# Squares added on GpSimd, and modulation weights in column blocks over interleaved partitions

## The reference, cut to what matters

```
c_act = silu(c)
for l in range(2):                                    # first block
    mod = c_act @ ada_w[l] + ada_b[l]                 # [1024] @ [1024, 9216]
    sh1, sc1, g1, sh2, sc2, g2, sh3, sc3, g3 = split(mod, 9)
    x = x + 0.5 * g1 * swiglu(modulate(rms_norm(x, norm_ffn1[l]), sh1, sc1), ...)
    x = x + g2 * token_mix(modulate(rms_norm(x, norm_mix[l]), sh2, sc2), ...)
    x = x + 0.5 * g3 * swiglu(modulate(rms_norm(x, norm_ffn2[l]), sh3, sc3), ...)
x = rms_norm(x, final_norm)
for i in range(2):                                    # second block, x and a context of 256 tokens
    mx = split(silu(c_2) @ ada_w_2[i] + ada_b_2[i], 6)
    mc = split(silu(c_ctx_2) @ ada_w_2[i] + ada_b_2[i], 6)
    ... attention (i = 0) or a gated linear recurrence, "LRU" (i = 1), then an MLP
```

## Time and profile before

| | before |
|---|---|
| Three runs, us | 2224.69, 2228.17, 2229.52 |
| Median, us | 2228.17 |
| Span of the profiled execution, us | 2222.6 (the page gives no other time for it) |
| PE, PEld busy | 97%, 90% |
| DVE, ACT, POOL busy | 75%, 45%, 1% |
| Moved by DMA | 417.47 MB, mean 188 GB/s |

### The profile page before, as it was taken

How to read it: one execution, slowest core, us unless ns; L and a number is a source line. 1 busy time by engine, 2 the same in 40 slices (tenths; PEclk the granted TensorE clock), 3 DMA queues, 4 the chain that set the end, 5 groups by cost and what they waited for, 6 DMA issues and landing times.

```text
span 2222.6 us, 36384 instructions
## 1 busy us (share of the span) xinstructions
PE 2155.5 (97%) x15539; PEld 1993.2 (90%) x15539; DVE 1674.6 (75%) x2327; ACT 990.5 (45%) x1331; POOL 31.1 (1%) x33
## 2 busy tenths in 40 slices
PE   7999999999999999999999899999999999999998
PEld 7999987999999998799998678888888887889998
DVE  6999877788798877778776774777776568987563
ACT  4534434534443443443344664422222348764442
POOL 0000000000000000000000000000000001110000
PEclk9999999999999999999999999999999999999999
DMA  9999744798789864467774102254465232133662
GB/s 322 317 330 309 248 133 150 242 316 298 264 284 305 302 202 153 142 196 248 236 228 142 36 4 74 80 186 155 156 221 189 76 114 69 48 122 127 223 191 76
DMA packets 338631, 417.47 MB, mean 188 GB/s; under 512 B 9274, under 2 KB 263208, under 8 KB 338472
## 3 DMA queue, kind: packets, MB, share of 16 engines
q1 hardware_dynamic: 335360, 411.84, 56.2%
q10 hardware_dynamic: 3112, 3.33, 0.5%
HBM read 414.09 MB, written 1.05 MB: 187 GB/s over the span
## 4 chain that ended last, share of the span: by engine, by line
PE 46%; DVE 7%; ACT 3%; issue 2%; POOL 0%; DVEq 0%; ACTq 0%
PE pb L623 45%; ACT wh L1461 1%; DVE wl L2100 1%; DVE T L2108 1%; PE pb L1289 1%; DVE ACC L2108 1%; DVE SM L2694 1%; DVE RS L2192 0%; DVE Hl L2108 0%; DVE L_y L2108 0%; ACT A_P L1935 0%; DVE L_y L2100 0%; ACT L_y L1462 0%; DVE L_y L2815 0%; DVE L_u L2108 0%
## 5 line engine op out<-in xcount | busy, mean ns | idle before, releaser
L623 PE MATMUL pb<-Hh,wh 128*128 128x256 f32 (+1 forms) x2624 | 795.5, 304 | 13.8 <-DVE wl L2100 5.4
L623 PE MATMUL pb<-Hl,wh 128*128 128x256 f32 (+1 forms) x2624 | 779.3, 297 | 0.0
L623 PE MATMUL pb<-Hh,wl 128*128 128x256 f32 (+1 forms) x2624 | 774.7, 297 | 0.0
L2100 DVE TENSOR_TENSOR wl<-raw,wh 128x2048 fp32r<-128x2048 f32 (+3 forms) x271 | 600.9, 2222 | 179.9 <-ACT wh L1461 179.1
L1461 ACT ACTIVATE wh<-raw 128x2048 fp32r<-128x2048 f32 (+3 forms) x271 | 502.2, 1855 | 357.6 <-PE pb L623 259.0
L623 PEld LDWEIGHTS pb<-Hh,wh 128*128 128x128 f32 x2624 | 504.6, 192 | 33.5 <-issue 9.6
L623 PEld LDWEIGHTS pb<-Hl,wh 128*128 128x128 f32 x2624 | 504.9, 192 | 15.3 <-issue 2.2
L623 PEld LDWEIGHTS pb<-Hh,wl 128*128 128x128 f32 x2624 | 501.9, 192 | 12.8
L623 PE MATMUL pb<-Bh,wh 128*128 128x256 f32 (+1 forms) x1376 | 420.1, 305 | 7.1 <-DVE Y L2100 2.5
L623 PE MATMUL pb<-Bl,wh 128*128 128x256 f32 (+1 forms) x1376 | 413.5, 300 | 0.0
L623 PE MATMUL pb<-Bh,wl 128*128 128x256 f32 (+1 forms) x1376 | 413.4, 300 | 0.0
(11 more groups left out here) (256 smaller groups left out, 2113.9 us busy)
## 6 DMA issues: line engine op xcount, KB each, us to landing
raw<-in_ada_w_dram SPq DMA_DIRECT2D x126, 1024.0 KB, 5.5
raw<-in_ffn_w_in_dram SPq DMA_DIRECT2D x88, 1024.0 KB, 6.7
raw<-in_mlp_w_dram SPq DMA_DIRECT2D x64, 1024.0 KB, 5.3
raw<-in_ffn_w_out_dram SPq DMA_DIRECT2D x32, 1024.0 KB, 6.5
raw<-in_mix_w_in_dram SPq DMA_DIRECT2D x22, 1024.0 KB, 5.7
raw<-in_ffn_w_out_dram SPq DMA_DIRECT2D x16, 768.0 KB, 4.6
raw<-in_attn_w_qkv_dram SPq DMA_DIRECT2D x12, 1024.0 KB, 6.2
raw<-in_lru_w_in_dram SPq DMA_DIRECT2D x10, 1024.0 KB, 5.1
```

The source lines that it names most:

```text
L623: return e.matmul(o, l, r, start=st, stop=sp, skip_group_check=True)
L2100: return e.tensor_tensor(o, a, b, f)
```

## The change

Two things change.

The squares of the first block: at a seam GpSimd adds the squares of tiles 0 to 5 (with 512 columns, 0 to 3) into one tile, and PE sums this tile and those of the rest: 3 matmuls instead of 8 (5 instead of 8). All of them now stand where tiles 6 and 7 did. The context's eight squares become one. ACT waits for GpSimd's additions before it reuses a slot.

The modulation: all segments but the first two are read so that a piece holds q column blocks of 512, block j on the partitions j, j + q, j + 2q, ... (q = 4: two neighbouring segments with the same due point; q = 2: one segment). A piece covers 512 / q rows and is loaded by q DMAs. The scalars for it (`CW`) come from 6 more small transposes in the opening of copies that DVE has widened. A flush comes once for 2q pieces and multiplies by q columns of ones and zeros, one for each block.

```diff
+FOLD_SLOT = (4, 5, 6, 7, 5, 6, 7, 5)
+FOLDED = {256: 6, 512: 4}
...
+        q = 2
+        if order and order[0] == (b, l, s + 1, *only) and due[order[0]] == due[seg]:
+            order.pop(0)
+            q = 4
+        for i in range(2 * q):
+            rows = w[512 // q * i:512 // q * (i + 1)]
+            adas.append(Piece(b, l, s, 0, q, i, vecs, due[seg], [rows[:, s * 1024 + 512 * j:s * 1024 + 512 * j + 512] for j in range(q)]))
...
+                if kind == "a":
+                    n = 128 // u.q
+                    for j, src in enumerate(u.parts):
+                        e.dma_start(view[j::u.q, :, :], src.rearrange("(k p) n -> p k n", p=n)).then_inc(sems[f"raw{p % RAW}"], 16)
+                    continue
...
+                blocks = KM[:, K_BLK[u.q]:K_BLK[u.q] + u.q]
                 for h in range(4):
-                    ins = mm(PB[7][:, c0 + h:c0 + h + 1], ACC[:, a, h * 128:h * 128 + 128], KM[:, K_ONE:K_ONE + 1], True, True)
+                    ins = mm(PB[7][:, c0 + h:c0 + h + 4 * u.q - 3:4], ACC[:, a, h * 128:h * 128 + 128], blocks, True, True)
...
+                    for i, kt in enumerate((0, *range(FOLDED[self.n], 8))):
+                        if i:
+                            E.wait_ge("sq", q0 + kt + 1)
+                        else:
+                            E.wait_ge("fold", f0 + FOLDED[self.n] - 1)
+                        E.mark(mm(self.p[:, 0:self.n], ONES, T[:, FOLD_SLOT[kt], 0:self.n], i == 0, kt == 7), "fold.read")
...
+            E.wait_ge("dve.step", 3)
+            pw = fill("su")
+            for a in range(6):
+                z = VW4[:, 128 * a:128 * a + 128] if a < 4 else VW2[:, 128 * a - 512:128 * a - 384]
+                ins = e.transpose(pw[:, 24 * a:24 * a + 24], z, KM[0:24, K_ID:K_ID + 24])
+            full(ins, "su")
             direct_cols(1)
...
+            def folded_square(kt, src, n, gained=False):
...
+                if kt > 3 and kt - 3 < folded:
+                    E.wait_ge("fold", E.n["fold"] - (folded - 1) + kt - 3)
+                elif kt > 3:
+                    E.wait_ge("fold.read", E.n["fold.read"] - (9 - folded) + kt - 3 - folded + 2)
+                z = T[:, FOLD_SLOT[kt], :]
+                if gained:
+                    act(z[:, n:2 * n], src, ACT.Square, scale=vt("n_fin", kt, 1))
+                act(z[:, 0:n], src, ACT.Square).then_inc(sems["sq"], 1)
...
+                    act(CW[:, :], full("su")[:, 0:144], ACT.Silu).then_inc(sems["su.read"], 1)
...
+            E.wait_ge("l_c", 64)
+            for q, z in ((4, VW4), (2, VW2)):
+                E.step(e.tensor_copy(z.rearrange("r (p q) -> r p q", q=q), VR[1][0:24, :].unsqueeze(2).to_broadcast([24, 128, q])))
...
+            def add_squares(dst, src, k):
+                E.wait_ge("sq", k)
+                E.wait_ge("fold", E.n["fold"])
+                E.mark(e.tensor_tensor(dst, dst, src, ALU.add), "fold")
```

More of the change, by code:

```diff
@@ L1 @@
 import itertools
-from collections import defaultdict
+from collections import defaultdict, namedtuple
 from contextlib import ExitStack
@@ L206 @@
 SUMS_BANK = 6
+FOLD_SLOT = (4, 5, 6, 7, 5, 6, 7, 5)
+FOLDED = {256: 6, 512: 4}
 LO_BANKS = {0: (0,), 1: (1,), 2: (2,), 3: (3, 4)}
 LO_FULL = {j: 2 * LO_STEPS.index((j, 1)) for j in range(4)}
+Piece = namedtuple("Piece", "b l s half q i vecs due parts")
 class Side:
@@ L239, in build @@
     adas, direct = [], []
-    for seg in sorted(due, key=lambda s: (due[s], s)):
+    order = sorted(due, key=lambda s: (due[s], s))
+    while order:
+        seg = order.pop(0)
         b, l, s, *only = seg
@@ L264, in build @@
     room = np.concatenate([[0.0], np.cumsum(at_unit)])
-    cost = np.cumsum([len(a[2]) for a in adas])
+    cost = np.cumsum([len(a.vecs) for a in adas])
     ends = {}
     for a, c in zip(adas, cost):
-        ends[a[3]] = c
+        ends[a.due] = c
     stream, ai, budget, sent = [], 0, 0.0, 0
@@ L272, in build @@
         budget = max(budget + max(rate, 0.0) * (room[i + 1] - room[i]), ends.get(i, 0))
-        while ai < len(adas) and (cost[ai] <= budget + 1e-6 or adas[ai][3] <= i):
+        while ai < len(adas) and (cost[ai] <= budget + 1e-6 or adas[ai].due <= i):
             stream.append(("a", adas[ai]))
@@ L876, in ffn @@
                 mods((0, 0, l, seg), (0, 0, l, seg + 1))
-                sums.add()
+                if seg or l:
+                    sums.add()
                 if between:
@@ L884, in ffn @@
                     if kind == "in":
-                        if first and (c, j) == (0, 3):
+                        if first and (c, j) == (1, 0):
                             csum = Sums(256)
-                            for kt in range(8):
-                                E.wait_ge("sq", E.up("sq"))
-                                mm(csum.p[:, 0:256], ONES, c_slot(kt), kt == 0, kt == 7).then_inc(sems["sq.read"], 1)
+                            E.up("sq", 8)
+                            E.wait_ge("fold", E.up("fold", 7))
+                            E.mark(mm(csum.p[:, 0:256], ONES, c_slot(0), True, True), "fold.read")
                         if first and (c, j) == (2, 0):
@@ L908, in ffn @@
                     if c == last:
-                        sums = Sums(512 if l and seg else 256)
+                        sums = Folded(512 if l and seg else 256)
                     for m in range(4):
@@ L913, in ffn @@
                         fm("fo", "fo", hid_at(b), 256, hid_need, said="x", by=2)
-                        if c == last and m:
-                            sums.add(2 * m)
                 return sums
@@ L1218, in _ @@
             sums.add()
-            SQUARES["first"] = E.n["sq"]
+            SQUARES["first"] = E.n["fold.read"]
             cx_rest(between)
@@ L1504, in square @@
                 nsq[0] += 1
+            def folded_square(kt, src, n, gained=False):
+                folded = FOLDED[512 if gained else 256]
+                if kt == 0:
+                    E.up("fold", folded - 1)
+                    E.up("fold.read", 9 - folded)
+                if kt == 6:
+                    act(SM[:, 25:26], KM[:, K_ONE:K_ONE + 1], ACT.Sqrt)
+                if kt > 3 and kt - 3 < folded:
[6 more added lines that the diff above has]
+                act(z[:, 0:n], src, ACT.Square).then_inc(sems["sq"], 1)
             def root_mean(n):
@@ L2255, in ffn @@
                     if kind == "in":
-                        if first and (c, j) == (1, 1):
+                        if first and (c, j) == (1, 2):
                             E.wait_ge("rs.sqrt", E.up("rs.sqrt"))
@@ L2625, in _ @@
             E.step(tt(S_GX, S_GX, vt("n_fin"), ALU.mult))
-            E.wait_ge("sq.read", SQUARES["first"])
+            E.wait_ge("fold.read", SQUARES["first"])
             E.step(ts(RS[:, 0:256], PB[SUMS_BANK][:, 0:256], EPS / D, EPS * EPS, ALU.mult, ALU.add))
@@ L2900, in _ @@
             for l in range(2):
+                folded(256)
                 for b in range(2):
@@ L2903, in _ @@
                     barred(l, b)
+                folded(256)
+                folded(512 if l else 256)
             for j in range(5):
```

126 lines of the change are left out of this document (77 added, 49 removed).

## The result

The changed kernel takes 2206.27 us in the median of 4 runs (2199.24 to 2211.57), the kernel before 2226.43 (2220.85 to 2229.52): ratio 0.9918, interval 0.9895 to 0.9940, about 20 us faster. Forecast were 2183 us and a range of 2172 to 2200. The sign is right; less than half of the 45 us came.

A forecast was written before the change was run, and what follows sets the result against it. The prediction took TensorE as the bound where its matmuls are dense, with DVE and loads close behind from 46 to 236 us. Terms: 32.4 + 12.9 + 4.0 - 0.9 - 3.0 = 45.4 us, forecast 2183 us, range 2172 to 2200.

The forecast's parts named there:

- Flushes outside the first block (32.4 us): Where PE is dense, outside 46 to 236 us: 40 of 48 removed flushes at 0.81 us each give 32.4 us.
- Squares (12.9): At the seams, fewer sums of squares on PE: four at 2.15 us, the first 1.7, the 512-column one 2.6; together 12.9.
- the lock (3.0): 35 new GpSimd additions and DVE's two-input SBUF instructions exclude each other: 3 us lost, between 0 and 12.
- In 46 to 236 us PE is relieved ... I take 4 us: 46 to 236 us: PE loses 9.5 us of work; with DVE near its limit 4 us gained, between 0 and 9.5.
- DVE's work stays 174.8 us: 46 to 236 us: DVE's work unchanged, its busy share at most 0.95 to 0.97, so 180 to 184 us against 190.
- Rival 1: DVE or loads take over; PE's relief between 46 and 805 us becomes waiting: 2197 us, chance 0.13.
- Four VectorE instructions a piece: Modulation sums: the new order keeps 1 MB pieces and four DVE instructions per vector, so a due group's cost is unchanged.
- I take nothing: SP queue: 280 more load issues fit between weight loads, cost nothing; upper end 1.53 us per q = 4 piece.
- rival 3: Interleaved part loads of 80 and 40 pieces not hidden: 143 us, 2326 us; decides from 45 us; chance 0.07.
- The opening (-0.9): Opening: six small transposes before the direct columns delay PE's first flushes by 0.9 us, bounds 0 and 1.5.
- All terms at their ends: Whole kernel: the prediction's own range, 2174 to 2191 us, said to put every term at its end.
- the second rival: Slow GpSimd additions or the DVE-GpSimd lock make each of six seams 2 us longer: 2195 us, chance 0.07.

The follow-up runs named there:

- column blocks alone: Changed kernel's column blocks over the partitions, all squares summed by TensorE as in the kernel before, no GpSimd addition: 2214.86 us, 0.9950 to the kernel before.
- additions alone: GpSimd adds the squares as in the changed kernel; modulation weights loaded and summed as in the kernel before, no six transposes: 2214.78 us, 0.9953.
- short flushes: Kernel before with one matmul instead of four in each of twelve flushes at 93 to 235 us, some values wrong: 2225.22 us, 1.0005.
- four transfers, interleaved: Kernel before with every 1 MB modulation piece loaded by four 256 KB transfers to every fourth partition: 2232.12 us, 1.0033.
- whole rows: Kernel before with every 1 MB modulation piece loaded by four 256 KB transfers of 128 whole rows to all 128 partitions: 2226.93 us, 1.0013.
- changed, transposes moved: Changed kernel with its six opening transposes placed behind the opening's flushes: 2203.78 us, 0.9904 to the kernel before.
- context's squares on TensorE: Changed kernel with the context's eight squares summed by TensorE as before, no GpSimd additions there: 2202.04 us, 0.9897 to the kernel before.
- early segments whole: Changed kernel with modulation segments due in the first 46 weight blocks in whole 1 MB pieces, summed as before: 2201.27 us, 0.9890.
- with both edits: Changed kernel with whole pieces for segments due in the first 46 weight blocks and the context's eight squares summed by TensorE: 2198.37 us, 0.9879.
- all three: Changed kernel with early segments in whole pieces, context's squares summed by TensorE, and six transposes behind the opening's flushes: 2192.55 us, 0.9851.
- one boundary later: The same three edits to the changed kernel, whole pieces going on to segments due at the 50th weight block: 2187.81 us, 0.9835.

## Why the prediction was wrong

**Flushes outside the first block (32.4 us): right in price, two too many.** 0.81 us each, 27 flushes left. But two flushes, not four, remained in the first block, so 38 went outside it: 30.8 us. Blocks alone shorten the rest by 26.4 us, and 3.0 us more are lost there at half clock than before (23.9 against a mean of 20.9): 29.4 without that, if a lost microsecond costs one. In the dense stretch from the 55th to the 121st weight half (417.6 to 808.7 us before) 21 flushes became 5 and one seam lies in it: 16 x 0.81 + 2.15 = 15.1 us; measured 391.1 to 375.9, 15.2.

**Squares (12.9) and the lock (3.0): the first right, the second not needed after the first block.** Additions alone: 14.2 us in the rest, 12.1 with equal lost clock. At the seams GpSimd is the one that waits, not VectorE, in the changed kernel:

```profile
601.81 2.28 DVE L2176 TENSOR_TENSOR wl<-raw,wh 128x2048 fp32r<-128x2048 f32 x1
602.03 3.55 POOL L2970 TENSOR_TENSOR T<-T 128x256 f32<-128x256 f32 x2 [3.14 <-ACT T L1518]
```

Of these two additions the first takes 2.67 us and ends after the `wl` row, the second 0.74. The chain of small instructions at 79 us is the case in which VectorE loses, once per addition. The Trainium skill, "SBUF — State Buffer", section "Who interferes with whom", says that whoever issues first holds the shared ports for the whole instruction; by that rule, the trace agrees: one long VectorE instruction costs GpSimd once, seven short additions cost VectorE seven times. I had the rule and priced it as an average of 0.5 us spread over idle time, where the place decides.

**"In 46 to 236 us PE is relieved ... I take 4 us": this step failed.** Its nature was wrong, not only its size: the block became 11.5 us longer. TensorE isn't the bound there; 7.3 us less work gave nothing. Of the 11.5 us, 7.0 are VectorE's busy time (an instruction held up by GpSimd counts as busy) and 4.5 its waiting. From the 1st to the 35th `wl` end, kernel by kernel:

| kernel | length, us | VectorE busy | the rest of the length |
|---|---|---|---|
| before, 4 profiles | 203.3 | 188.3 | 15.0 |
| short flushes | 203.3 | 188.4 | 15.0 |
| additions alone | 207.0 | 192.0 | 15.0 |
| four transfers, interleaved / whole rows | 207.7 / 206.0 | 189.1 / 188.6 | 18.6 / 17.4 |
| column blocks alone | 210.6 | 191.8 | 18.8 |
| changed, 3 profiles | 214.8 | 195.3 | 19.5 |
| changed, transposes moved | 215.0 | 196.0 | 19.0 |
| context's squares on TensorE | 211.5 | 192.2 | 19.3 |
| early segments whole / with both edits | 208.8 / 207.2 | 193.0 / 189.8 | 15.9 / 17.3 |
| all three / one boundary later | 205.6 / 203.6 | 189.5 / 188.5 | 16.0 / 15.1 |

The additions lengthen VectorE's time and leave its waiting alone; four transfers do nearly the reverse; the changed kernel has both. I wrote "DVE's work stays 174.8 us" and let its busy share rise. The work did not stay and the share did not rise (188.3 of 203.3 us before, 195.3 of 214.8 after). Rival 1 had the right mechanism in too small a place: relief becomes waiting up to 250 us, and not between 403 and 805, where all of it came.

**Four VectorE instructions a piece, "DVE's work stays": failed in the column blocks.** The number stayed, the kind didn't. The first product of an accumulator is a TENSOR_SCALAR, the later ones a SCALAR_TENSOR_TENSOR, which takes longer. Before, an accumulator began every second piece, now every 2q. All of them before, and those in column blocks of the changed kernel, with min/median/max in ns:

```profile
L2108 DVE SCALAR_TENSOR_TENSOR ACC<-raw,SM,ACC x525: 740/752/769, 8.1 to 2168.6; 128x512 f32<-128x512 f32 x175
L2104 DVE TENSOR_SCALAR ACC<-raw,SM x75: 386/481/494, 7.6 to 2127.7; 128x512 f32<-128x512 f32 x75
...
L2184 DVE SCALAR_TENSOR_TENSOR ACC<-raw,CW,ACC x552: 652/751/1767, 66.2 to 2148.3; 128x512 f32<-128x512 f32 x184
L2180 DVE TENSOR_SCALAR ACC<-raw,CW x24: 478/481/483, 65.7 to 2026.8; 128x512 f32<-128x512 f32 x24
```

In the first block 15 of the short kind became 5: 10 x 0.27 = 2.7 us of the 3.5 by which VectorE is busier with the blocks alone. No run changes this kind alone, so it is an account of the rows and not an experiment.

**"I take nothing" for the issues: failed, by 4.4 us.** The bound of 1.53 us a piece came from four LRU loads in 1.9 us; a part to every fourth partition is issued in 0.60 to 0.65, four in 2.55. SyncE's queue has little to draw on: from 50 to 250 us of the kernel before it waits 176.8 us for VectorE to free a buffer (total, times, longest):

```profile
SPq L568 <- DVE ACC L2108: 112.2, 29, 8.6
SPq L568 <- DVE wl L2100: 64.6, 33, 4.5
```

Even so, most of the added issue time is hidden: 29 pieces there at 2.18 us more each are 63 us, and the block of the kernel before grew by 4.4. Of that 3.6 us are VectorE's waiting, against 4.5 in the changed kernel and 3.8 with the blocks alone, so the form of the transfers accounts for most of the waiting. It never reached the 45 us of rival 3: in the rest, kernels with the split pieces are not longer.

**The context's additions: missed.** They are in no term but the relief: +3.7 us in place of -3.0 (7 x 0.43).

**The opening (-0.9): right** at the late fall of the clock.

**The clock: no term for it.** The changed kernel loses 11.0 us more at half clock over its span (42.2 against 31.1 in the means): 6.7 in the first block, 3.0 in the rest, the remainder in the opening and at the end. In the rest, where TensorE is the bound, 38.5 + 3.0 = 41.5 us is what would have come without it, against 42.3 forecast. In the first block part of it follows the gap at 86 us and goes with it (3.4 us lost there with the context's squares on TensorE, 7.9 in the mean of the changed kernel). Why it falls oftener was not tried.

**The range.** "All terms at their ends" would be 31.8 to 54.8 us of gain, 2173 to 2196, and not 2174 to 2191; the measured 2206 lies outside either. The lock is the mechanism of the second rival, not of the third, as the prediction calls it.

In the stages, then, the forecast missed by 15.5 us in the first block, 3.8 in the rest and some 0.5 in the opening. The other 5.5 of the 25 us are the difference between profiles (25.7 us between the mean spans) and timed runs (20.2): the four profiled runs of the kernel before had a granted clock of 0.985 to 0.987, its timed runs 0.989 in the median.

## What to carry to other kernels

A busy TensorE row is no proof of a bound: work taken off it was worth nothing in a stretch where VectorE was busy for 0.93 of the time and the transfers stood at 0.95. Price such a stretch by VectorE and by its loads, and count for VectorE the kind of each instruction and not only their number. With few buffers the parts of a split load are not free, though most of their issue time is hidden, so split a load only in stretches with room. An addition moved to GpSimd should not run beside a chain of short VectorE instructions that something waits for. No run here takes VectorE's work or the loads in that stretch below those of the kernel before, so how much either would give is open.

## What was not expected of the hardware

- A transfer of 256 KB to every fourth partition mostly takes 0.60 to 0.65 us of SyncE's queue, one to 128 partitions 0.45, a 1 MB one 0.37 to 0.59.
- The opening's granted clock falls at 28 to 32 us or at 34 to 36 us, both in executions of the same program. TensorE is busy from 29 to 33 us in either case. The early fall makes 5 us.
- VectorE's TENSOR_SCALAR of 256 columns with one tensor input takes 0.29 us alone and 0.72 beside GpSimd's additions.
- VectorE's TENSOR_SCALAR of 512 columns in fp32 takes 0.48 us, its SCALAR_TENSOR_TENSOR 0.75.
- After 4 us with TensorE busy 0.55 us, 7 us at half clock follow. Without the additions before it both are gone, and the first block is 3.3 us shorter.
